# Moving the rounding and splitting of the mLSTM state C ahead of the weight splits, and two small pieces of work to other places

## Time and profile before

| | value |
|---|---|
| median of 3 runs | 1510.87 us |
| profiled execution | 1510.56 us, span 1509.1 us |
| PE busy | 1486.6 us, 99% |
| DVE busy | 935.5 us, 62% |
| ACT busy | 664.4 us, 44% |
| POOL busy | 184.5 us, 12% |
| window 575 to 1175 us (the heads but their first 17 us): PE, DVE, ACT busy | 592.0, 462.0, 307.8 us |
| granted PE clock in that window | 1.00 |

### The profile page before, as it was taken

How to read it: one execution, slowest core, us unless ns; L and a number is a source line. 1 busy time by engine, 2 the same in 40 slices (tenths; PEclk the granted TensorE clock), 3 DMA queues, 4 the chain that set the end, 5 groups by cost and what they waited for, 6 DMA issues and landing times. The chain is left out here.

```text
span 1509.1 us, 31633 instructions
## 1 busy us (share of the span) xinstructions
PE 1486.6 (99%) x11131; PEld 1472.1 (98%) x11131; DVE 935.5 (62%) x1617; ACT 664.4 (44%) x949; POOL 184.5 (12%) x331
## 2 busy tenths in 40 slices
PE   9999999999999999999999999999999999999996
PEld 9999999999999999999999999999999999999996
DVE  7756565554444458787777777786868554544444
ACT  6433433433333335454545555545455433333442
POOL 4000000001000002213030303031312000000000
PEclk9999999999999999999999999999999999999998
DMA  7765555557556577696959595959697556565543
GB/s 233 208 163 147 175 151 173 157 165 223 181 175 182 175 206 175 187 254 163 278 152 288 145 292 146 284 152 281 158 274 173 197 175 182 169 183 192 172 154 140
DMA packets 310006, 289.62 MB, mean 192 GB/s; under 512 B 82728, under 2 KB 297456, under 8 KB 309168
## 3 DMA queue, kind: packets, MB, share of 16 engines
q1 hardware_dynamic: 291424, 243.05, 57.7%
q0 software_dynamic: 18288, 45.97, 8.9%
q10 hardware_dynamic: 256, 0.10, 0.0%
HBM read 263.62 MB, written 25.42 MB: 192 GB/s over the span
## 5 line engine op out<-in xcount | busy, mean ns | idle before, releaser
L1088 DVE TENSOR_TENSOR wlo<-raw,whi 128x1024 fp32r<-128x1024 f32 x416 | 507.2, 1222 | 494.9 <-ACT whi L811 494.0
L439 PE MATMUL ps<-xh,whi 128*128 128x288 f32 x2560 | 760.5, 297 | 0.0
L441 PE MATMUL ps<-xh,wlo 128*128 128x288 f32 x2560 | 755.2, 295 | 0.0
L440 PE MATMUL ps<-xl,whi 128*128 128x288 f32 x2560 | 754.1, 295 | 0.0
L811 ACT ACTIVATE whi<-raw 128x1024 fp32r<-128x1024 f32 x416 | 440.5, 1060 | 711.9 <-PE ps L441 691.2
L439 PEld LDWEIGHTS ps<-xh,whi 128*128 128x128 f32 x2560 | 481.0, 188 | 0.3
L441 PEld LDWEIGHTS ps<-xh,wlo 128*128 128x128 f32 x2560 | 480.6, 188 | 0.0
L440 PEld LDWEIGHTS ps<-xl,whi 128*128 128x128 f32 x2560 | 480.3, 188 | 0.2
L440 PE MATMUL ps<-yl,whi 128*128 128x288 f32 x512 | 151.6, 296 | 0.0
L441 PE MATMUL ps<-yh,wlo 128*128 128x288 f32 x512 | 150.9, 295 | 0.0
L439 PE MATMUL ps<-yh,whi 128*128 128x288 f32 x512 | 150.1, 293 | 0.0
(11 more groups left out here) (361 smaller groups left out, 1289.5 us busy)
## 6 DMA issues: line engine op xcount, KB each, us to landing
raw<-in_w_in_dram SPq DMA_DIRECT2D x320, 512.0 KB, 3.9
raw<-in_w_pb_dram SPq DMA_DIRECT2D x32, 512.0 KB, 3.6
Cin<-in_state_mlstm_C_dram POOLq DMA_DIRECT2D x16, 1024.0 KB, 8.7
Xb<-in_state_mlstm_C_dram SPq DMA_DIRECT2D x256, 64.0 KB, 3.8
out_dram<-Cin POOLq DMA_DIRECT2D x16, 1024.0 KB, 6.3
raw<-in_w_pa_dram SPq DMA_DIRECT2D x32, 512.0 KB, 3.5
raw<-in_w_out_dram SPq DMA_DIRECT2D x32, 512.0 KB, 3.6
part_d<-part POOLq DMA_DIRECT2D x8, 288.0 KB, 3.2
```

What stands on the lines that cost most here:

```text
L439: nc.tensor.matmul(out, whi[:, c, kk, cols], mh_[:, k, :], start=(k == 0), stop=False)
L440: nc.tensor.matmul(out, whi[:, c, kk, cols], ml_[:, k, :], start=False, stop=False)
L441: last = nc.tensor.matmul(out, wlo[:, c, kk, cols], mh_[:, k, :], start=False, stop=(k == KT - 1))
L1088: nc.vector.tensor_tensor(wlo[:, c], raw[:, c], whi[:, c].bitcast(F32), ALU.subtract).then_inc(lo_ready, 1)
```

## The change

`ct_copy` copies the two columns of n as well, on ACT, ahead of C's rounding; `ct_split` loses that copy. In both loops ACT does `ct_copy` ahead of `split_hi`, and DVE does `ct_split` and the turn ahead of `split_lo`. The turns of sequences 0 and 1 stand at chunk 2 of the loop before (0 was at its end, 1 in the v loop at chunk 0). n's sums move from chunk 3 of the v loop to chunk 1 of the o loop.

```diff
@@ ct_copy (ACT)
+            nc.scalar.activation(CTh[:, :, DH:DH + 2], nT[:, :, ds(h + 8 * b, 1), :].squeeze(2).bitcast(F32), ACT.Copy)
             nc.scalar.activation(CTh[:, :, 0:DH], of_c(b), ACT.Copy).then_inc(ct_ev, 1)
@@ ACT, v loop
             for c in range(CHUNKS):
+                ct_copy(h, c)
                 split_hi(H0 + 3 + 5 * h, c)
-                ct_copy(h, c)
@@ ACT, o loop
             for c in range(CHUNKS):
+                ct_copy(h, 4 + c)
                 split_hi(H0 + 4 + 5 * h, c)
-                ct_copy(h, 4 + c)
@@ ct_split (DVE)
             dve.wait_ge(ct_ev, 8 * h + b + 1)
-            nc.vector.tensor_copy(CTh[:, :, DH:DH + 2], nT[:, :, ds(h + 8 * b, 1), :].squeeze(2).bitcast(F32))
@@ DVE, loop before the v loop
+                if c == 2:
+                    turn_blocks(h, 0)
+                    turn_blocks(h, 1)
                 if c == 3:
                     ...
-                    turn_blocks(h, 0)
@@ DVE, v loop
             for c in range(CHUNKS):
+                ct_split(h, c)
+                if c > 0:
+                    turn_blocks(h, c + 1)
                 split_lo(H0 + 3 + 5 * h, c)
-                ct_split(h, c)
-                turn_blocks(h, c + 1)
@@ DVE, end of chunk 3 of the v loop: n's sums (L1474 to L1486) taken out
@@ DVE, o loop
+            for c in range(CHUNKS):
+                ct_split(h, 4 + c)
+                if c < 3:
+                    turn_blocks(h, 5 + c)
+                split_lo(H0 + 4 + 5 * h, c)
+                if c == 2:
+                    dve.wait_ge(v_ev, h + 1)
+                    nc.vector.tensor_copy(kv4[:, 1]...).then_inc(kv4_set, 1)
+                if c == 0:
+                    ... the scores' weights, as before (p_set)
+                if c == 1:
+                    ... n's sums (nn_ev)
-            for c in range(CHUNKS):
-                split_lo(H0 + 4 + 5 * h, c)
-                if c == 2:
-                    ... kv4[:, 1], as above
-                ct_split(h, 4 + c)
-                if c < 3:
-                    turn_blocks(h, 5 + c)
```

More of the change, by code:

```diff
@@ L1473, in _ @@
                                           bc(qk[:, 2:4, TP:T], 2, [P, 2, P // S, S])).then_inc(kv4_set, 1)
+            for c in range(CHUNKS):
[5 more added lines that the diff above has]
+                    dve.wait_ge(v_ev, h + 1)
+                    nc.vector.tensor_copy(kv4[:, 1].rearrange("p j (n s) -> p j n s", s=S),
+                                          bc(vz[:, :, TP:T], 2, [P, 2, P // S, S])).then_inc(kv4_set, 1)
+                if c == 0:
+                    dve.wait_ge(s_mm, h + 1)
+                    dve.wait_ge(w_exp, h + 1)
+                    nc.vector.scalar_tensor_tensor(W[:, 0:384], ps[:, 5, 0:384], DH ** -0.5, W[:, 0:384],
+                                                   ALU.mult, ALU.mult)
+                    nc.vector.tensor_copy(W[S:2 * S, 384:416], ident[S:2 * S, S:2 * S])
+                    nc.vector.scalar_tensor_tensor(W[0:S, 384:416], ps[0:S, 5, 384:416], DH ** -0.5,
+                                                   W[0:S, 384:416], ALU.mult, ALU.mult).then_inc(p_set, 1)
+                if c == 1:
                     dve.wait_ge(wsb_set, h + 1)
@@ L1486, in _ @@
                     nc.vector.tensor_tensor(of_head, of_head, added, ALU.add).then_inc(nn_ev, 1)
-            for c in range(CHUNKS):
-                split_lo(H0 + 4 + 5 * h, c)
-                if c == 2:
-                    dve.wait_ge(v_ev, h + 1)
-                    nc.vector.tensor_copy(kv4[:, 1].rearrange("p j (n s) -> p j n s", s=S),
-                                          bc(vz[:, :, TP:T], 2, [P, 2, P // S, S])).then_inc(kv4_set, 1)
-                ct_split(h, 4 + c)
-                if c < 3:
-                    turn_blocks(h, 5 + c)
[L1497 to L1504, removed]
                 if c == 3:
```

## The result

| | before | after |
|---|---|---|
| median | 1510.79 us (9 runs, 1510.35 to 1511.14) | 1514.95 us (9 runs, 1514.66 to 1515.89) |
| ratio | | 1.0028, 95% interval 1.0018 to 1.0039 |
| profiled execution | 1510.56 us | 1514.99 us, span 1513.5 us |

A forecast was written before the change was run, and what follows sets the result against it. PE was taken to bound the kernel, busy 99% of the span, so only its waits could move. 8 heads by 0.58 is 4.6, less 0.3: +4.3 us on 1510.56, 1515.2 us as median; 8 in 10 range 1508.5 to 1519.5.

The forecast's parts named there:

- The old waits go: v part: PE's waits at `inter` 0 to 2, with restarts 1.61 us per head, all vanish.
- A wait of 0.57 ahead of the scores: PE ahead of L654: DVE's copy now stands behind subtraction, turn and split_lo; new wait 0.57 us, head 1.20 ahead there.
- A wait of 0.62 ahead of L671: o part: the second kv4 copy now stands behind the subtraction; new PE wait 0.62 us, head 0.58 ahead.
- the restart: PE after a stop: starting again costs some 0.10 us beyond the wait; 0.10 was added ahead of `inter` 6.
- v's turns 5.13 us behind `inter` 6: PE ahead of L685: ACT's split now precedes the four copies; turns at 931.67 instead of 931.09, head 0.58 us behind.
- Nothing behind that point: After v's turns: nothing changes order, so heads lie 79.7 us apart instead of 79.1.
- the one longer wait that is swallowed: One `inter` wait lasted 0.8 us instead of 0.46; such an early excess is now swallowed: -0.3 us.
- The small copy at 0.15: n's copy on ACT: step 0.10 us plus 0.05 for its register address, 0.15 each; bounds 0 and 0.35.
- the third chain: From PE's `inter` 6 through ACT's rounding, split and four copies to v's turns: 5.13 us where 3.79 is free.
- The wash: Rival: the small copy's 0.15 comes to nothing, three chains get 0.45 us shorter: 1511.6 us; 0.27 for all within 0.2%.
- the three chains: Steps from PE's `inter` to scores, L671 and v's turns: 3.88, 3.92 and 5.13 us, over the free 3.31, 3.31, 3.79.
- All waits vanish: Rival: the three `inter` waits go and none comes, 1497.7 us; chance 0.15 together with an in-between case of about 1507.

The follow-up runs named there:

- e1: Changed kernel with both kv4 copies placed ahead of ct_split instead of behind split_lo: 1503.76 us, ratio 0.9953 to the kernel before.
- e2: Changed kernel with chunk 3 of the o loop in the old order on ACT and DVE (weight split first): 1507.40 us, ratio 0.9979.
- e3: Changed kernel with n's two columns copied by DVE again, as before the change: 1514.99 us, ratio 1.0029 to the kernel before.
- e7: Changed kernel with the edits of e1 and e2 together: 1495.97 us, ratio 0.9903 to the kernel before.
- e8: e7 with DVE starting after the first two of ACT's four copies and PE waiting for the other two itself: 1494.40 us, ratio 0.9893.
- e6: Kernel before with only turns 0 and 1 moved to chunk 2 of the loop before the v loop: 1501.16 us, ratio 0.9938.
- e5: Changed kernel with the whole o loop in the old order on ACT and DVE: 1501.81 us, ratio 0.9943 to the kernel before.

## Why the prediction was right, point by point

- **The old waits go, 1.61 us per head.** Right. All eight heads have 0.13 or 0.14 ahead of `inter` 0, 1 and 2. The rounding of C on ACT follows PE's last L604 by 906.92 - 906.32 = 0.60, where 0.58 was worked out; its two terms were both off, see the small copy below.
- **A wait of 0.57 ahead of the scores.** It measured 0.62. e1 shows that it hangs on the copy's place behind the subtraction, the turn and split_lo. L654 starts 0.99 later than before in a head that began 2.12 later, so the head is 1.13 ahead there, where 1.20 was worked out.
- **A wait of 0.62 ahead of L671.** It measured 0.62, and e1 takes it away too. The head is 0.52 ahead behind it, not 0.58, and the restart there costs 0.05 (0.85 from L671 to the last L604, 0.80 before), not 0.10. These two errors cancel by luck, and v's turns come 0.58 late as worked out.
- **v's turns 5.13 us behind `inter` 6.** 933.79 - 928.67 = 5.12. e2 shows that the weight split on ACT and DVE in this one chunk makes the difference.
- **Nothing behind that point, heads 79.7 us apart.** From v's turns to `inter` 0 of the next head it is 48.20 us, and before 48.82 with the old wait of 0.62 in it. The first operation on DVE in the fifth and the sixth head:

```profile
875.18 0.39 DVE L1402 TENSOR_SCALAR bcrow<-nb,eye 128x320 fp32r<-128x320 f32 x1 [0.55 <-DVE Cin L1397]
954.88 0.39 DVE L1402 TENSOR_SCALAR bcrow<-nb,eye 128x320 fp32r<-128x320 f32 x1 [0.55 <-DVE Cin L1397]
```

  They are 79.70 apart. Eight times 0.58 and the one longer wait that is swallowed made +4.3; +4.2 was measured.
- **The small copy at 0.15.** Too small, and the term ahead of it was too long by as much. The 0.43 from PE's last L604 to ACT's rounding (927.02 to 927.45 in the earlier trace rows) was not the time that ACT needs to follow PE, since ACT was still in its weight split (926.49, step 0.96). Where ACT does wait, the rounding follows by 0.38. So it is in the kernel before (L604 at 901.23) and in e3 (L604 at 923.88):

```profile
901.61 0.63 ACT L930 ACTIVATE CTh<-Yb 128x512 fp32r<-128x512 f32 x1 [0.20 <-PE ps L604]
...
924.26 0.64 ACT L930 ACTIVATE CTh<-Yb 128x512 fp32r<-128x512 f32 x1 [2.52 <-PE ps L604]
```

  In the changed kernel the small copy starts 0.48 behind L604 (928.67 to 929.15) and the rounding 0.59. So the copy puts the rounding off by 0.21: 0.11 is its step, and 0.10 comes ahead of it, where the prediction had 0.05 for the register. The sum has 0.43 + 0.15 = 0.58 for what is 0.38 + 0.21 = 0.59, right by luck. In the third chain e3 gives 0.19 per head for it.
- **The wash.** It needed the copy to cost nothing, and the 0.21 rule that out. But e3 also shows that the copy is no dearer on ACT than on DVE over the whole kernel: with it back on DVE the three chains are as late together. So the order of the steps made the waits, and not the copy's engine.
- **"All waits vanish": three chains would have to be shorter.** Right as a condition, and it can be met by order alone, without a shorter operation: in e1 for the first two chains, in e7 nearly for the third too (0.39 is left, and 0.15 in e8).

What the prediction did not see is how little of the change was needed. It took the change as one thing. Split by the runs, each relative to its own runs of the kernel before: the early turns alone bring -9.3 us (e6); the new order in the v loop, n's copy and the sums' place add +0.7 (e5 against e6, from one set); the new order in the o loop adds +12.8 (the changed kernel against e5). Together this is the +4.2 of the result. The shares hold for this sequence of kernels; neither loop's new order was run on the kernel before by itself.

## What to carry to other kernels

When work is put ahead of something that an engine used to do in its idle time, that something does not vanish: it lands behind the next release, in front of whatever stood there, so follow every later item of the loop to its reader, not only the one that is moved forward. Put an operation that needs nothing into idle time first (the early turns), and put the shortest operation that somebody waits for ahead of the long one (the 0.28 us copy ahead of the 1.2 us split). An order that helps in one chunk of a loop need not be right for the others: here the gain lay in three `inter`, and the loss in the two kv4 copies and in chunk 3 of the o loop.

## What was not expected of the hardware

A stop of PE costs more than the time waited. The prediction had 0.10 for it: the first L602 behind a stop starts its successor 0.22 us later (900.77 to 900.99 before), and 0.12 later without a stop (905.96 to 906.08 after). But the price hangs on the matmuls that start there. From the first L654 to L657 it is 1.41 after the stop (913.92 to 915.33) and 1.30 in e1, without it (907.66 to 908.96). From L671 to L672 it is 0.16 (927.82 to 927.98) and in e1 0.11 (920.84 to 920.95). With these 0.16 the two bare waits of 0.62 make 1.40 per head and 11.2 us in all, which is what e1 brought.

A 4-element cast on DVE behind a release from ACT put off what follows it by 0.19 to 0.27 us (e3, o loop of the fifth head: the subtraction started 0.22 to 0.30 behind the rounding's end, against 0.03 without the cast), though the cast's own step in a busy stretch was 0.06. Why, no run shows.
